# An MoE stage's overflow blocks: from one block at a time to a pipelined loop body

## What is computed

```
def grouped_experts(x, expert, weights, w_gate, w_up, w_down):
    ...
    def expert_block(args):
        xs, e = args
        return (jax.nn.silu(xs @ w_gate[e]) * (xs @ w_up[e])) @ w_down[e]
    yb = lax.map(expert_block, (xb, blk_e)).reshape(n_blocks * MOE_BLOCK, D)
    y = yb[dest] * sw[:, None].astype(yb.dtype)
    return jax.ops.segment_sum(y, tok, num_segments=T)
```

## Time and profile before

| | |
|---|---|
| median of 3 runs | 2328.67 us |
| the profiled execution | 2326.66 us |
| its span | 2324.9 us |
| mean granted TensorE clock | 0.891 |
| TensorE busy (matmul rows) | 1941.5 us, 84% |
| VectorE busy | 1305.1 us, 56% |
| ScalarE busy | 1078.6 us, 46% |
| DMA | 443.06 MB, mean 191 GB/s |

### The profile page before, as it was taken

How to read it: one execution, slowest core, us unless ns; L and a number is a source line. 1 busy time by engine, 2 the same in 40 slices (tenths; PEclk the granted TensorE clock), 3 DMA queues, 4 the chain that set the end, 5 groups by cost and what they waited for, 6 DMA issues and landing times. The chain is left out here.

```text
span 2324.9 us, 28234 instructions
## 1 busy us (share of the span) xinstructions
PE 1941.5 (84%) x10249; PEld 1536.3 (66%) x10249; DVE 1305.1 (56%) x1954; ACT 1078.6 (46%) x1671; POOL 225.8 (10%) x203
## 2 busy tenths in 40 slices
PE   7899987999978888865976999389999999995640
PEld 2899766999866777720525555278888888874530
DVE  1534324544455677751001366589888889864427
ACT  5311114444266777720110221268887887763324
POOL 0100000000012334300100000001000000000002
PEclk9999997999967999977785899699999999997775
DMA  8411128542145000018581722189999999975517
GB/s 274 114 51 53 65 78 264 225 154 83 40 134 167 19 15 6 5 39 241 142 182 53 270 95 83 51 327 415 426 414 418 413 413 416 409 303 215 222 49 281
DMA packets 155006, 443.06 MB, mean 191 GB/s; under 512 B 37073, under 2 KB 82005, under 8 KB 123209
## 3 DMA queue, kind: packets, MB, share of 16 engines
q1 hardware_dynamic: 135785, 340.78, 39.7%
q0 software_dynamic: 13792, 81.90, 10.4%
q10 hardware_dynamic: 5328, 19.02, 2.0%
HBM read 387.17 MB, written 58.70 MB: 192 GB/s over the span
## 5 line engine op out<-in xcount | busy, mean ns | idle before, releaser
L2719 DVE TENSOR_TENSOR moe_lo<-wts_raw,moe_hi 128x2048 fp32r<-128x2048 f32 x216 | 484.3, 2287 | 59.5 <-ACT moe_hi L2634 59.4
L2634 ACT ACTIVATE moe_hi<-wts_raw 128x2048 fp32r<-128x2048 f32 x216 | 401.2, 1915 | 25.2 <-PE moe_U L2516 25.2
L2502 PE MATMUL moe_G<-moe_hi,moe_xh 128*128 128x512 f32 x288 | 117.8, 409 | 43.2 <-DVE moe_lo L2719 35.5
L872 PE MATMUL cmp_hp<-cmp_xh,cmp_wh 128*128 128x256 f32 (+2 forms) x512 | 151.0, 295 | 0.0
L948 DVE TENSOR_TENSOR cmp_xl<-cmp_bank,cmp_xh 128x512 fp32r<-128x512 f32 (+1 forms) x136 | 82.6, 668 | 121.5 <-ACT cmp_xh L902 121.4
L872 PE MATMUL cmp_hp<-cmp_xh,cmp_wl 128*128 128x256 f32 (+2 forms) x512 | 147.5, 288 | 0.0
L872 PE MATMUL cmp_hp<-cmp_xl,cmp_wh 128*128 128x256 f32 (+2 forms) x512 | 147.4, 288 | 0.0
L1361 POOL TENSOR_SCALAR att_prow<-att_prow,att_scale 128x640 f32<-128x640 f32 (+15 forms) x96 | 113.7, 1197 | 339.4 <-DVE att_scale L1485 339.4
L1458 DVE TENSOR_TENSOR att_pl<-att_pT,att_ph 128x512 fp32r<-128x512 f32 (+5 forms) x148 | 101.3, 688 | 79.5 <-ACT att_ph L1389 79.1
L2542 PE MATMUL moe_Y<-moe_hi,moe_hh 128*128 128x512 f32 x288 | 118.4, 411 | 29.4 <-DVE moe_hl L2735 24.9
L1962 POOL DMA_INDIRECT rou_xg<-s_h,rou_idx x36 | 51.3, 1425 | 882.9 <-PE moe_XT L2521 538.6
(11 more groups left out here) (448 smaller groups left out, 4458.5 us busy)
## 6 DMA issues: line engine op xcount, KB each, us to landing
wts_raw<-in_w_gate SPq DMA_DIRECT2D x72, 1024.0 KB, 7.1
wts_raw<-in_w_up SPq DMA_DIRECT2D x72, 1024.0 KB
wts_raw<-in_w_down SPq DMA_DIRECT2D x72, 1024.0 KB
s_yb<-moe_y ACTq DMA_DIRECT2D x36, 512.0 KB, 7.9
smp_wa<-in_w_ada SPq DMA_DIRECT2D x8, 2048.0 KB
fro_wraw<-in_w_ada SPq DMA_DIRECT2D x4, 2048.0 KB
s_yb<-att_zero SPq DMA_DIRECT2D x1, 8192.0 KB
fro_wraw<-in_w_in SPq DMA_DIRECT2D x12, 512.0 KB
```

The costliest lines, as they stand in the source:

```text
L872: last = pe.matmul(hp[u % 2][:, 0:n], lhs[:, w, :], rhs[:, u % 3, at], start=(r == 0 and t == 0 and m == 0), stop=(r == 1 and t == 7 and m ...
L2502: pe.matmul(G[:, :], xh[k][:, c, :], wh, start=(c == 0), stop=False)
L2634: act.activation(hi[p][half][:, :], raw[p][half][:, :], ACT.Copy).then_inc(hi_ready[p], 1)
L2719: dve.tensor_tensor(lo[p][half][:, :], raw[p][half][:, :], hi[p][half][:, :], ALU.subtract).then_inc(lo_ready[p], 1)
```

## The change

The further blocks get a pipeline too. In the body `more` of block `n`, TensorE now does `turn_x(n)`, `down(n-2)`, `gate(n)`, `turn_h(n-1)`, `up(n)`; VectorE makes `hidden(n-1)`, the down split and the `h_copy` of block `n-1` between or after the splits of block `n`; ScalarE copies out and stores block `n-2`. The last turn of `expert` (block 31) leaves its unfinished work to the first body, and behind the loop `final`, a register with the number of the last block, closes the last two blocks. The wait on the store after every block goes; the stores of these blocks use one buffer `y[0]` and a semaphore `y_more`, on which the next copy into that buffer waits. SyncE's and GpSimd's code stays as it is. No matmul, split, load or store is added or dropped.

```diff
         def overflow(eng, body):
...
+            return blocks + (NE - 1)
...
                 up(pe, k, n)
-                if before:
+                if before and following:
                     down(pe, n - 1)
...
             expert(NE // 2 - 1, 1, following=False)
-            turn_h(pe, NE - 1)
-            down(pe, NE - 1)
 
             def more(b, k, n, i):
                 pe.wait_ge(x_in[k], 16 * i + 16)
                 pe.wait_ge(xl_ready, n)
                 turn_x(pe, k)
+                down(pe, n - 2)
                 gate(pe, k, n)
+                turn_h(pe, n - 1)
                 up(pe, k, n)
-                turn_h(pe, n)
-                down(pe, n)
-
-            overflow(pe, more)
+
+            final = overflow(pe, more)
+            down(pe, final - 1)
+            turn_h(pe, final)
+            down(pe, final)
...
+            def y_last(n):
+
+                act.wait_ge(y_done, n + 1)
+                act.wait_ge(y_more, 16 * (n - NE + 3))
+                act.activation(y[0][:, 0:512], Y[0][:, :], ACT.Copy)
+                act.activation(y[0][:, 512:D], Y[1][:, :], ACT.Copy).then_inc(y_a, 1)
+
+            def store_last(n):
+                act.wait_ge(y_a, n + 1)
+                act.dma_start(a["s_yb"][bass.ds(n * P, P), :], y[0][:, :]).then_inc(y_more, 16)
 
             def more(b, k, n, i):
+                split(GATE, n)
                 x_copy(k, n)
-                split(GATE, n)
                 split(UP, n)
+                y_last(n - 2)
+                split(DOWN, n - 1)
+                store_last(n - 2)
                 silu(n)
-                split(DOWN, n)
-                h_copy(n)
-                y_copy(k, n, i)
-                store(k, n, n)
-                act.wait_ge(y_out[k], 16 * i + 16)
-                act.activation(settled[:, :], ident[0:1, 0:1], ACT.Copy)
...
+                h_copy(n - 1)
...
+            final = overflow(act, more)
+            y_last(final - 1)
+            split(DOWN, final)
+            store_last(final - 1)
+            h_copy(final)
+            y_last(final)
+            store_last(final)
+            act.wait_ge(y_more, 16 * (final - NE + 4))
+            act.activation(token[:, :], ident[0:1, 0:1], ACT.Copy)
...
             def more(b, k, n, i):
+                split(GATE, n)
+                hidden(n - 1)
                 x_copy(k, n)
-                split(GATE, n)
                 split(UP, n)
-                hidden(n)
-                split(DOWN, n)
-                h_copy(n)
-
-            overflow(dve, more)
+                split(DOWN, n - 1)
+                h_copy(n - 1)
+
+            final = overflow(dve, more)
+            hidden(final)
+            split(DOWN, final)
+            h_copy(final)
```

More of the change, by code:

```diff
@@ L2415, in stage_experts @@
         y = [s.sb(f"y{i}", [P, D]) for i in range(2)]
-        settled = s.sb("settled", [1, 1])
+        token = s.sb("token", [1, 1])
         NP2 = 2 * TT
@@ L2471, in stage_experts @@
         y_out = [s.sem(f"y_out{i}") for i in range(2)]
+        y_more = s.sem("y_more")
         done_with = (g_done, u_done, y_done)
@@ L2675, in expert @@
                     split(UP, n + 1)
-                if before:
+                if before and following:
                     y_copy(1 - k, n - 1, i - 1 + k)
-                split(DOWN, n)
-                if before:
+                if following:
+                    split(DOWN, n)
+                if before and following:
                     store(1 - k, n - 1, n - 1)
@@ L2692, in _ @@
             expert(NE // 2 - 1, 1, following=False)
-            h_copy(NE - 1)
-            y_copy(1, NE - 1, NE // 2 - 1)
-            store(1, NE - 1, NE - 1)
+            def y_last(n):
[6 more added lines that the diff above has]
+                act.dma_start(a["s_yb"][bass.ds(n * P, P), :], y[0][:, :]).then_inc(y_more, 16)
             def more(b, k, n, i):
+                split(GATE, n)
                 x_copy(k, n)
-                split(GATE, n)
                 split(UP, n)
+                y_last(n - 2)
+                split(DOWN, n - 1)
+                store_last(n - 2)
                 silu(n)
-                split(DOWN, n)
-                h_copy(n)
-                y_copy(k, n, i)
-                store(k, n, n)
-                act.wait_ge(y_out[k], 16 * i + 16)
-                act.activation(settled[:, :], ident[0:1, 0:1], ACT.Copy)
-            act.wait_ge(y_out[0], 16 * (NE // 2))
-            act.wait_ge(y_out[1], 16 * (NE // 2))
-            overflow(act, more)
+                h_copy(n - 1)
+            act.wait_ge(y_out[0], 16 * (NE // 2 - 1))
+            act.wait_ge(y_out[1], 16 * (NE // 2 - 1))
+            act.activation(token[:, :], ident[0:1, 0:1], ACT.Copy).then_inc(y_more, 16)
+            final = overflow(act, more)
[7 more added lines that the diff above has]
+            act.activation(token[:, :], ident[0:1, 0:1], ACT.Copy)
         @block.vector
@@ L2821, in expert @@
                     split(GATE, n + 1)
-                hidden(n)
                 if following:
+                    hidden(n)
                     split(UP, n + 1)
-                split(DOWN, n)
+                    split(DOWN, n)
             expert(0, 0, before=False)
```

## The result

The changed kernel takes 2301.83 us in the median of 4 runs (2297.05 to 2308.02); the kernel before takes 2332.66 in 4 runs of its own (2326.91 to 2338.55). The ratio is 0.9869, with a 95% interval from 0.9828 to 0.9911: faster, by between 0.9% and 1.7%. I had forecast 2288, with a range of 2279 to 2301. The time lies 13.8 above the forecast and 0.8 above the range.

What follows compares the result with a forecast made beforehand. A chain of waits, no full engine, was taken to bound the further blocks. Lead-in to 2103.8, three periods of 26.3 and a tail of 35.5 put the last stage 40.3 us earlier: 2286.4, plus 2.0, predicted 2288, range 2279 to 2301.

Steps and rivals of the forecast that it cites:

- X: Moment in a further block's turn when the down buffer's first half is free, forecast 12.8 us after the second gate half lands.
- TensorE's wait for the skipped bodies: Behind the further blocks' loop: TensorE passes 12 skipped bodies before `down(34)`, 6.8 us with 3.9 covered, a cost of 2.8 us.
- Everything ahead is the same: Claim that nothing before SyncE issues block 32's gate load at 2079.66 us changes; only the 180.3 us to 2259.92 can.
- the 2286.4 of the sum: Forecast profiled execution: 2326.66 us before minus a gain of 40.3; the median of the runs was put 2.0 above.
- The lead-in: Start of block 32: second gate half lands near 2091.0, plus 12.8 of splits and subtractions, so X(32) = 2103.8.
- The first turn: First of three further-block periods, each forecast 26.3 us: 13.5 for loading and landing four weight halves, plus 12.8.
- The other two turns: Remaining two of three equal further-block periods, each forecast 26.3 us, 13.5 plus 12.8, bringing X(35) to 2182.7.
- The tail: After X(35): last gate, up, skipped bodies, two downs, store and token, forecast X + 35.5 = 2218.2; last stage at 2219.6.
- (a): Rival: loads run ahead and the new loop keeps the experts' 17.7 us pace, 25.8 us less, 2262; chance 0.07.
- (b): Rival: loads exposed in SyncE's queue cost more than the waits replaced; slower below 178 GB/s, 2342 at 150; chance 0.03.
- (c): Rival: smaller gain, bursts at some 240 GB/s or a similar further wait, period 33.7 us, time 2310; chance 0.03.
- (d): Rival: a register wait or the loop serialises the further blocks, nothing gained, 2329; chance 0.02.

## Why the prediction was right and wrong

**The mechanism was right.** The chain that closes a turn is the one that I named: down load at X, gate behind it, landing, 12.8 of splits and subtractions, next X. The splits and subtractions measured 13.2, 12.7 and 12.7 (from the start of the second gate split to X). The cause, the queue order, was tested by the loads that run ahead: turns of 17.8. TensorE's wait for the skipped bodies was there (3.07, forecast 2.8), ScalarE's bodies moved under it (1.3 left of 5.45, forecast 1.4), the splits and `moe_h` came in the order of the rows.

**The base was wrong.** "Everything ahead is the same" is true of the code, not of one execution's time. I added up from one profile and took the median of three runs, 2328.67, as the kernel's time; ten later runs gave 2335.26. The split is exact on profiles: the changed kernel's first one took 21.6 more than the 2286.4 of the sum, 6.2 of it in T (gain 34.1 for 40.3) and 15.4 in the rest (2155.4 for 2140.0). Its second profile took 2300.96, 14.6 more: 7.0 in T and 7.5 in the rest. So half or more of the miss is no cost of the change. With 2335.26 as the base the same sum would have come to 2295.0, 4 under the 2299.03 of the runs beside it. My range had no term for this scatter: that is the step that failed. It needed the terms below as well. The upper end lay 13 above the forecast, and the 6.2 of the stage alone, or the rest of the 13.8 alone, would have stayed inside.

**Four terms were mis-sized**, all on the same side, 6.3 together (25.52 + 81.79 + 38.88 for 24.1 + 78.9 + 36.9):

- The lead-in: +1.4. The second gate half was split 12.35 after its issue, not 11.3, and its chain took 13.2. What made this landing late wasn't tried.
- The first turn: +2.3. The second gate half was split 15.9 after X, not 13.5. In the 13.5 I had given the store a share and the gather of block 35 none. The Trainium skill's rule on semaphore writes ("DMA: Bandwidth & Descriptors", "Queues, rings and completion order") pointed the right way, with an estimated 1.3 for the gather; the run with the late gather took 1.3 to 1.8 of the landing and as much of the turn away. That delay is shown; whether it comes by that rule or by shared bandwidth isn't.
- The other two turns: +0.3 each, from splits that start 13.9 after X. Part of this was luck. I took 13.5 because the burst would be issued at once and keep the queue full; it was not, and DMA moved only 237 GB/s until the gate issue and 382 behind it, in the rows above, where I had 414. The 2.5 that I had added for the landing and the store took up most of this.
- The tail: +2.0. `gate` took 8.5 for 7.7 and `up` ended at X + 8.1 for X + 7.0; the gap was 0.3 longer, and the two `down` took 0.6 more together (5.9 for 5.5, 8.3 for 8.0). TensorE had been idle for 6.0, ran most of `gate` at the lower clock (granted 0.50, 1.2 GHz) and only the last 2.5 at the full one (2.4 GHz), as the view by stretch shows below. The 7.7 that I took was less than the 8.1 of the row that I had, and no row gave me that reduction.

```profile
2197.18:2203.25 6.07, 6.07 (x14) 4.77 (x15) 6.07 (x3) 5.19 (x5) 0.00 (x0) 0.50 0.21 86
2203.25:2205.70 2.45, 2.45 (x13) 2.03 (x12) 2.45 (x2) 0.00 (x0) 0.00 (x0) 1.00 0.43 90
```

On the branches, the Trainium skill's figure of about 108 ns ("Advanced Engine Details and Errata", "Control Flow Timing") fell against the row again: 208 to 210 ns on TensorE, and without six of them the gap shrinks by 2.2. My sentence that the pass would hide wholly by that figure was wrong too: 19 branches at 0.108 instead of 0.21 leave an estimated 4.9 of the 6.8, more than the 3.9 that I had as covered.

**The rivals.** (a), the experts' pace, can't come from this change, but its price was near: the run with the loads ahead has it, at 2269.64 where I had 2262 (2268.6 with 2335.26 as the base). (b), exposed loads slower than 178 GB/s, and (c), a period of 33.7, did not occur: the four halves had landed 13.9 to 15.9 after X. Nor did (d).

## What to carry to other kernels

When a loop is made to overlap its iterations, the loads have to be re-ordered with it: a load that waits for its buffer holds back every later load of the same queue, and here that order held back another 31 us, nearly as much as the whole change gave in T (34). Compare kernels between fixed events of the trace and not by whole times of one profile: here T repeated within 0.8 us in two profiles of one kernel, while the rest of the span moved by 8 and by 10. And where a loop skips bodies, ask which engine passes the branches while others wait for it.

## What was not expected of the hardware

- Two executions of one program differ by 10 us in when a stage begins (2079.66 and 2089.68) and by 0.2 in how long it takes. All of it is there at the gate load of block 1 (1509.30 and 1519.47); what in the stages ahead does it was not settled.
- The landing of one 0.5 MB store: 2.6 behind its issue when nothing else is queued, some 8.7 when DMA is busy all the time (2077.72 to 2086.44).
- A gather of 0.5 MB, issued 5.9 after X on another queue, made the gate load of that turn land 1.3 to 1.8 later.
- A skipped body's compare-and-branch takes a median of 208 ns on TensorE, but 45 on ScalarE and SyncE and 56 on VectorE, in the changed kernel's first profile.
